# HGRN-2 decay levels: copies of the three widest levels moved to ScalarE, two levels formed in their valid blocks only

## The chip, the cores and the metric

The kernel runs on one core of a Trainium2 chip. The metric is the device time of one execution in microseconds. Three runs of the kernel before took 1720.81, 1721.70 and 1721.91 us (median 1721.7).

## The reference

Two blocks of a language model run over 256 tokens of width 1024 in float32: a Mamba-style mixer with a PEER layer, then a block with an HGRN-2 mixer, a convolutional FFN, windowed attention and a second FFN. The change lies in the HGRN-2 mixer. What it must compute, for each of 8 heads (q, k, v from the projections, `logf` the log of the forget gate):

```python
def step(state, inp):
    qb, kb, vb, gb = inp
    cum = jnp.cumsum(gb, axis=2)
    o_inter = jnp.einsum('bhtk,bhkv->bhtv', qb * jnp.exp(cum), state)
    rel = cum[:, :, :, None, :] - cum[:, :, None, :, :]
    decay = jnp.exp(jnp.where(causal, rel, -jnp.inf))
    scores = jnp.einsum('bhtk,bhsk,bhtsk->bhts', qb, kb, decay)
    o_intra = jnp.einsum('bhts,bhsv->bhtv', scores, vb)
    ...
```

So token t reads token s with the weight sum over k of q[t,k] k[s,k] exp(cum[t,k] - cum[s,k]).

## The kernel before

The 256 tokens are two tiles of 128. Scores are formed transposed (s on the partitions, t on the columns), as a hierarchy of **levels**, so that each exponent is taken against a reference point between s and t. Level 0 is the tile level: queries of tile 1 against keys of tile 0. Levels 1 to 7 have spans m = 64, 32, 16, 8, 4, 2, 1: within each run of 2m tokens the second half reads the first. Level 8 is the diagonal. They run in `LEVEL_ORDER` = 8, 0, 1, 2, ..., 7.

Work of one level x, on four engines that only meet at semaphores:

- **VectorE** `differences(x)` writes the exponents of the query side and the key side (two operations of 1024 columns, lines 2086 and 2088) into `QK[x % 2]`; it waits until TensorE has finished level x-2, which used the same buffer.
- **ScalarE** `level_exp(x)` takes both exponentials (lines 1970 and 1971).
- **VectorE** `q_side(x)` multiplies the query half by q (line 2123).
- **TensorE** `level(x)` (line 1855) forms a full 128x128 product for each of the 16 pairs of head and tile, though only the blocks of that level are valid, in banks 4 to 7, four to a bank; a float32 product shows as two matmul records. Level 0 is 8 products in banks 4 and 5 (line 1846). `bank_free` holds a bank until the level before has been copied out of it.
- **VectorE** `take(x)` (line 2139) copies each bank into `PP` under the mask of that level, four copies of 128x512; for level 0 it is two plain copies into `CR` (line 2132). Each adds to `level_out`.

Between the levels TensorE does slabs 2 to 13 of a weight stream, `wide(k)`: 12 matmuls of 512 columns (lines 320 to 322), tabled in `AFTER`. A slab comes from HBM into a ring of four and is split in two parts: **ScalarE** `split(k)` (line 239) writes the rounded high part of the slab that `wide(k + 3)` will use, **VectorE** `split(k)` (line 247) the rest. The high part of a slot may be overwritten only when TensorE has finished the slab that was there, so ScalarE's `split(k)` waits for the end of `wide(k - 1)`. At k = 8 ScalarE first copies four finished banks out (line 2005, `VT`), after `wide(7)`.

All queues are in order and written by hand. ScalarE's order per level x is: the splits up to `max(AFTER[x]) + 1`, then `level_exp(x + 2)`. VectorE's is: first split of `AFTER[x]`, `take(x)`, `q_side(x + 1)`, `differences(x + 2)`, remaining splits. When the last level is copied out, `read_out` (line 1877) forms the outputs.

Of the kernel before, what the change touches and what calls it, by code (L numbers as in the profile page):

```python
# [14 lines left out]
F32 = mybir.dt.float32  # L15
# [3 lines left out]
ACT = mybir.ActivationFunctionType  # L19
# [3 lines left out]
P = 128  # L23
# [108 lines left out]
def build(nc, t):  # L132
    ctx = ExitStack()
    with ctx:
# [16 lines left out]
        iota = sb("iota", P)  # L151
        tiny = sb("tiny", 64)
        arena = sb("arena", 32768)
        bank = [ctx.enter_context(nc.psum_tensor(f"bank{i}", [P, 512], F32)) for i in range(8)]

        def V(name, i=0, n=1):
            o = VEC[name][0]
# [147 lines left out]
                    last = short(k, k == KT - 1)  # L305
            last.then_inc(slabs_done, 1)

        def up_wide(pe, n0, k, bank_free=None):


            q = slot(n0 + k, 0)
            pe.wait_ge(lo_ready, n0 + k + 1)
            for tt in range(TT):
                x = slice(k * SEQ + tt * P, k * SEQ + (tt + 1) * P)
                for nh in range(2):
                    if bank_free is not None:
                        pe.wait_ge(bank_free, 2 * tt + nh + 1)
                    o = bank[2 * tt + nh][:, :]
                    w = slice(q * 1024 + nh * 512, q * 1024 + (nh + 1) * 512)
                    nc.tensor.matmul(o, xhi[:, x], whi[:, w], start=k == 0, stop=False)  # L320
                    nc.tensor.matmul(o, xhi[:, x], wlo[:, w], start=False, stop=False)
                    last = nc.tensor.matmul(o, xlo[:, x], whi[:, w], start=False, stop=k == KT - 1)  # L322
            last.then_inc(slabs_done, 1)

        def down_half(o, y, nh, q, first):

# [1487 lines left out]

        LEVEL_ORDER = (8, 0, 1, 2, 3, 4, 5, 6, 7)
        AFTER = {8: (2,), 0: (3,), 1: (4, 5), 2: (6, 7), 3: (8, 9), 4: (10,), 5: (11, 12), 6: (), 7: (13,)}
        PLACE_OF = {x: at for at, x in enumerate(LEVEL_ORDER)}

        def span_of(x):
            return ((P,) + LEVELS[:-1])[x]  # L1820

        def pe_hgrn(pe):
            turn_pe(pe, T_HG)
            up(pe, N_HG, U_HG, 0, 0, 4, SEQ, x_ready=lo_base(T_HG))
            steps(pe, 15, 4, lambda i, r: up(pe, N_HG + 1, U_HG + 1, i, r, 4, SEQ))

            def wide(k):
                up_wide(pe, N_HG + 16 + k // 8 * 8, k % 8, s("v_out") if k == 8 else None)

            def level(x):  # L1830

                before = LEVEL_ORDER[PLACE_OF[x] - 1] if PLACE_OF[x] else None
                if x < 8:
                    pe.wait_ge(s("qk_q"), x + 1)
                    pe.wait_ge(s("e_k"), x + 1)

                def bank_free(b):
                    if before is not None:
                        pe.wait_ge(s("level_out"), 4 * PLACE_OF[x] - 4 + (4 if before == 0 else b + 1))

                qk = QK[x % 2]
                if x == 0:
                    for hd in range(HG_H):
                        if hd % 4 == 0:
                            bank_free(hd // 4)
                        nc.tensor.matmul(bank[4 + hd // 4][:, (hd % 4) * P:(hd % 4 + 1) * P],
                                         qk[:, hd * SEQ:hd * SEQ + P], qk[:, hd * SEQ + P:(hd + 1) * SEQ],
                                         start=True, stop=True).then_inc(s("level_mm"), 2)
                    return
                for hc in range(2 * HG_H):  # L1850
                    if hc % 4 == 0:
                        bank_free(hc // 4)
                    q = slice(hc * P, (hc + 1) * P)
                    a, b = (KK[:, q], QQ[:, q]) if x == 8 else (qk[:, q], qk[:, q])
                    nc.tensor.matmul(bank[4 + hc // 4][:, (hc % 4) * P:(hc % 4 + 1) * P], a, b,  # L1855
                                     start=True, stop=True).then_inc(s("level_mm"), 1)

            pe.wait_ge(s("onr_in"), 16)
            nc.tensor.transpose(bank[7][:, 0:P], ONR, ident[:, :]).then_inc(s("onr_tr"), 1)
            pe.wait_ge(up_evac, U_HG + 16 + 2)  # L1860
            wide(0)
            wide(1)
            pe.wait_ge(s("q_silu"), 1)
            pe.wait_ge(s("onc"), 1)
            for x in LEVEL_ORDER:
                level(x)
                for k in AFTER[x]:
                    wide(k)
            pe.wait_ge(s("level_out"), 4 * 9)

            def read_out(half):
                for tt in range(TT):
                    for hd in range(4 * half, 4 * half + 4):
                        o = bank[4 + 2 * tt + half][:, (hd % 4) * P:(hd % 4 + 1) * P]
                        v = lambda c: VT[:, c * D + hd * P:c * D + (hd + 1) * P]
                        if tt == 0:
                            last = nc.tensor.matmul(o, PP[:, hd * SEQ:hd * SEQ + P], v(0), start=True, stop=True)
                        else:
                            nc.tensor.matmul(o, CR[:, hd * P:(hd + 1) * P], v(0), start=True, stop=False)
                            last = nc.tensor.matmul(o, PP[:, hd * SEQ + P:(hd + 1) * SEQ], v(1),  # L1880
                                                    start=False, stop=True)
                    last.then_inc(s("o_mm"), 1)

            def wide_last(nh):

                for z in range(2):
                    n = N_HG + 16 + 14 + z
                    q = slot(n, 0)
                    if nh == 0:
                        pe.wait_ge(lo_ready, n + 1)  # L1890
                    w = slice(q * 1024 + nh * 512, q * 1024 + (nh + 1) * 512)
                    for tt in range(TT):
                        x = slice((6 + z) * SEQ + tt * P, (6 + z) * SEQ + (tt + 1) * P)
                        o = bank[2 * tt + nh][:, :]
                        nc.tensor.matmul(o, xhi[:, x], whi[:, w], start=False, stop=False)
                        nc.tensor.matmul(o, xhi[:, x], wlo[:, w], start=False, stop=False)
                        last = nc.tensor.matmul(o, xlo[:, x], whi[:, w], start=False, stop=z == 1)
                        if nh and tt:
                            last.then_inc(slabs_done, 1)
                        elif z:  # L1900
                            last.then_inc(s("gate_mm"), 1)

            def turned_out(half):
                pe.wait_ge(s("o_gated"), 2 * half + 2)
                for j in (0, 2, 1, 3):
                    for tt in range(TT):
                        c = tt * D + (4 * half + j) * P
                        last = nc.tensor.transpose(turned_y(4 * half + j)[:, tt * P:(tt + 1) * P],
                                                   OO[:, c:c + P], ident[:, :])
                    if j > 1:  # L1910
                        last.then_inc(s("o_tr"), 1)

            read_out(0)
            read_out(1)
            wide_last(0)
            wide_last(1)
            turned_out(0)
            down(pe, N_HGO, D_HGO, 0, 0, 4, first=True)
            down(pe, N_HGO + 1, D_HGO + 1, 0, 0, 4)
            turned_out(1)  # L1920
            for j in (2, 3, 4, 5):
                down(pe, N_HGO + j, D_HGO + j, 0, 0, 4)
            down_last(pe, N_HGO + 6, D_HGO + 6)
# [7 lines left out]
        def act_hgrn(act, chain):  # L1931
# [69 lines left out]
            def slot_free(k):  # L2001
# [4 lines left out]
                            .then_inc(s("v_out"), 1)  # L2006
                split(k)

            level_exp(0)
            split(0)  # L2010
            split(1)
# [2 lines left out]
            for x in LEVEL_ORDER:  # L2014
                while done <= max(AFTER[x], default=0) + 1 and done < 14:
                    slot_free(done)
                    done += 1
                if x + 2 < 8:
                    level_exp(x + 2)
            split(14)  # L2020
# [14 lines left out]
        def dve_hgrn(dve, chain):  # L2035
# [90 lines left out]
            def take(x):  # L2126

                at = PLACE_OF[x]
                if x == 0:
                    for b in range(2):  # L2130
                        dve.wait_ge(s("level_mm"), 16 * at + 8 * (b + 1))
                        nc.vector.tensor_copy(CR[:, b * 512:(b + 1) * 512], bank[4 + b][:, :])\
                            .then_inc(s("level_out"), 2)
                    return
                for b in range(4):
                    dve.wait_ge(s("level_mm"), 16 * at + 4 * (b + 1))
                    if at:
# [13 lines left out]
            for x in LEVEL_ORDER:  # L2151
                if AFTER[x]:
                    split(AFTER[x][0])
                take(x)
                if x < 7:
                    q_side(x + 1)
                if x + 2 < 8:
                    differences(x + 2)
                for k in AFTER[x][1:]:
# [655 lines left out]
```

## Time and profile before

| | |
|---|---|
| median of three runs | 1721.7 us |
| the profiled execution: time, span | 1720.77 us, 1719.0 us |
| TensorE (PE) busy | 1671.2 us, 97% of the span |
| PE weight loads, VectorE, ScalarE, GpSimd busy | 88%, 75%, 60%, 6% |
| chain that ended last | PE 89%, VectorE 4%, ScalarE 4%, issue 2%, DMA 1% |
| level stage (first wide slab to first output product) | 1135.0 to 1207.7 us |

PE is TensorE's matmuls, PEld its weight loads, DVE VectorE, ACT ScalarE. PEclk is the granted clock of TensorE as a share of 2.4 GHz; 0.50 is 1.2 GHz. A matmul's recorded duration is longer than the distance to the next start, because matmuls are pipelined: costs are read from start to start. Idle time in brackets counts from the end of the record before.

### The profile page before, as it was taken

Reading aid. Unit: us, or ns where it says so; the run is one execution under the profiler, and the core shown is the slowest. Engines: PE = TensorE matmul, PEld = TensorE weight load, DVE = VectorE, ACT = ScalarE, POOL = GpSimd, SP = SyncE. Lnnn points to the kernel's source line nnn. Section 1 sums busy time; section 2 is a strip of 40 time slices with the busy share of each in tenths; the row PEclk is TensorE's granted clock in tenths of the full one; section 3 lists DMA queues with packets and bytes.
Section 4 is the critical chain, followed back from the end, with each engine's and each line's share of the span. In section 5 each row is a group of like instructions: output and inputs, shape, how many; then the busy total and the mean of one; then the engine's idle time right before and its main releaser. Section 6 shows DMA issues by size and latency. Waiting matters only on the chain.

```text
span 1719.0 us, 34329 instructions
## 1 busy us (share of the span) xinstructions
PE 1671.2 (97%) x10835; PEld 1505.5 (88%) x10835; DVE 1285.0 (75%) x2348; ACT 1031.7 (60%) x1615; POOL 109.7 (6%) x100
## 2 busy tenths in 40 slices
PE   7999999999999999999999999999999998999997
PEld 6998889999999999988888888898788887778886
DVE  6876773799967777777777777789677777867776
ACT  7656554667556666655445544764575667666655
POOL 0014300344100000000000000000000000000000
PEclk9999999999999999999999999999999999999999
DMA  5552356578765555577787777543356554246653
GB/s 201 165 157 94 107 181 211 174 223 230 230 213 169 180 170 178 164 233 241 244 273 239 242 243 239 171 148 99 123 172 190 191 193 140 87 147 196 188 191 109
DMA packets 113261, 315.62 MB, mean 184 GB/s; under 512 B 12624, under 2 KB 44752, under 8 KB 112688
## 3 DMA queue, kind: packets, MB, share of 16 engines
q1 hardware_dynamic: 112352, 310.83, 56.4%
q0 software_dynamic: 848, 4.00, 0.7%
q8 instruction: 35, 0.57, 0.1%
q14 instruction: 26, 0.21, 0.0%
HBM read 296.43 MB, written 18.35 MB: 183 GB/s over the span
## 4 chain that ended last, share of the span: by engine, by line
PE 89%; DVE 4%; ACT 4%; issue 2%; DMA 1%; ACTq 0%; DVEq 0%; SPq 0%
PE bank L263 11%; PE bank L264 11%; PE bank L265 11%; PE bank L328 10%; PE bank L329 10%; PE bank L330 10%; PE bank L284 9%; PE bank L288 5%; PE bank L1397 3%; PE bank L1855 1%; ACT whi L239 1%; DVE wlo L247 1%; PE bank L320 1%; PE bank L322 1%; DVE h L479 1%
## 5 line engine op out<-in xcount | busy, mean ns | idle before, releaser
L247 DVE TENSOR_TENSOR wlo<-raw,whi 128x1024 fp32r<-128x1024 f32 x500 | 614.5, 1231 | 145.7 <-ACT whi L239 136.1
L239 ACT ACTIVATE whi<-raw 128x1024 fp32r<-128x1024 f32 x524 | 550.5, 1052 | 40.4 <-PE bank L322 34.4
L263 PE MATMUL bank<-x,whi 128*128 128x256 f32 (+1 forms) x1728 | 507.5, 294 | 6.0 <-DVE arena L798 1.7
L265 PE MATMUL bank<-x,wlo 128*128 128x256 f32 (+1 forms) x1728 | 491.5, 284 | 0.0
L264 PE MATMUL bank<-x,whi 128*128 128x256 f32 (+1 forms) x1728 | 491.1, 284 | 0.0
L263 PEld LDWEIGHTS bank<-x,whi 128*128 128x128 f32 x1728 | 331.1, 192 | 11.1 <-issue 8.6
L264 PEld LDWEIGHTS bank<-x,whi 128*128 128x128 f32 x1728 | 331.8, 192 | 0.1
L265 PEld LDWEIGHTS bank<-x,wlo 128*128 128x128 f32 x1728 | 331.0, 192 | 0.0
L328 PE MATMUL bank<-whi,yhi 128*128 128x512 f32 x816 | 319.5, 392 | 4.9 <-DVE ylo L2340 2.0
L329 PE MATMUL bank<-wlo,yhi 128*128 128x512 f32 x816 | 318.1, 390 | 0.0
L330 PE MATMUL bank<-whi,ylo 128*128 128x512 f32 x816 | 317.5, 389 | 0.0
L328 PEld LDWEIGHTS bank<-whi,yhi 128*128 128x128 f32 x816 | 153.4, 188 | 38.5 <-issue 5.3
L330 PEld LDWEIGHTS bank<-whi,ylo 128*128 128x128 f32 x816 | 153.2, 188 | 32.4
L329 PEld LDWEIGHTS bank<-wlo,yhi 128*128 128x128 f32 x816 | 153.4, 188 | 29.4
L284 PE MATMUL bank<-x,whi 128*128 128x512 f32 x704 | 177.4, 392 | 1.0 <-DVE x L601 0.8
L1481 ACT ACTIVATE yhi<-h 128x256 fp32r<-128x256 f32 x128 | 53.4, 417 | 170.9 <-PE bank L330 167.2
L284 PEld LDWEIGHTS bank<-x,whi 128*128 128x128 f32 x704 | 129.2, 188 | 27.2 <-issue 1.2
L1434 ACT ACTIVATE h<-bank 128x256 f32<-128x256 f32 x128 | 49.2, 384 | 150.1 <-PE bank L265 149.9
L1675 DVE TENSOR_TENSOR ylo<-h,yhi 128x256 fp32r<-128x256 f32 x128 | 54.4, 425 | 66.8 <-ACT yhi L1481 66.8
L288 PEld LDWEIGHTS bank<-x,wlo 128*128 128x128 f32 x704 | 96.9, 190 | 6.9
L288 PE MATMUL bank<-x,wlo 128*128 128x256 f32 x704 | 100.2, 282 | 0.0
L1630 DVE TENSOR_SCALAR h<-iota,h 128x128 f32<-128x128 f32 x256 | 76.9, 343 | 22.9 <-PE bank L1397 22.9
(323 smaller groups left out, 1705.0 us busy)
## 6 DMA issues: line engine op xcount, KB each, us to landing
raw<-in_stream SPq DMA_DIRECT2D x524, 512.0 KB, 3.5
act_spill<-h SPq DMA_DIRECT2D x124, 128.0 KB, 3.2
h<-act_spill SPq DMA_DIRECT2D x124, 128.0 KB, 3.3
h<-in_x SPq DMA_DIRECT2D x1, 1024.0 KB, 5.3
arena<-in_keys POOLq DMA_DIRECT2D x1, 1024.0 KB, 6.5
h_spill<-h SPq DMA_DIRECT2D x1, 1024.0 KB, 8.4
arena<-h_spill POOLq DMA_DIRECT2D x1, 1024.0 KB, 7.8
arena<-in_g_final POOLq DMA_DIRECT2D x1, 512.0 KB, 9.3
```

What stands on the lines that cost most here:

```text
L239: nc.scalar.activation(whi[:, q * 1024:(q + 1) * 1024], raw[:, q * 1024:(q + 1) * 1024], ACT.Copy).then_inc(hi_ready, 1)
L247: nc.vector.tensor_tensor(wlo[:, q * 1024:(q + 1) * 1024], raw[:, q * 1024:(q + 1) * 1024], whi[:, q * 1024:(q + 1) * 1024].bitcast(F32), ...
L263: nc.tensor.matmul(bank[b][:, 0:T], whi[:, w], xhi[:, x], start=k == 0, stop=False)
L264: nc.tensor.matmul(bank[b][:, 0:T], whi[:, w], xlo[:, x], start=False, stop=False)
L265: last = nc.tensor.matmul(bank[b][:, 0:T], wlo[:, w], xhi[:, x], start=False, stop=k == KT - 1)
L284: return nc.tensor.matmul(bank[b][:, :], whi[:, w], both, start=k == 0, stop=k == KT - 1)
L288: return nc.tensor.matmul(bank[b][:, SEQ:2 * SEQ], wlo[:, w], xhi[:, k * SEQ:(k + 1) * SEQ], start=False, stop=stop, skip_group_check=True)
L328: nc.tensor.matmul(o, yhi[:, y], whi[:, w], start=first, stop=False, skip_group_check=True)
L329: nc.tensor.matmul(o, yhi[:, y], wlo[:, w], start=False, stop=False, skip_group_check=True)
L330: return nc.tensor.matmul(o, ylo[:, y], whi[:, w], start=False, stop=True, skip_group_check=True)
L1630: nc.vector.tensor_scalar(HOT1[:, y % 2 * P:(y % 2 + 1) * P], iota[:, :], c1(I1T), c1(GT_COLS), ALU.is_equal, ALU.mult).then_inc(s("hot_a" ...
L1675: nc.vector.tensor_tensor(ylo[:, yq * SEQ:(yq + 1) * SEQ], PRD[:, yq * SEQ:(yq + 1) * SEQ], yhi[:, yq * SEQ:(yq + 1) * SEQ].bitcast(F32), ...
```

## The change

- The eight PSUM banks become slices of one PSUM tensor, so that one access can span banks 4 to 7 (`SCORES`).
- Levels 1 (m = 64) and 2 (m = 32) are formed only in their valid blocks: per head and tile, level 1 is one product of 64 weight columns and 64 moved columns at output partitions 0 to 63; level 2 is two products of 32 by 32, at output partitions 0 and 64. Both wait for all four banks before they start.
- The copies of levels 0, 1 and 2 go from VectorE's queue to ScalarE's: two of 512 columns for level 0 as before, one of 64 partitions by 1024 elements for level 1, two of 32 partitions by 512 elements for level 2. In ScalarE's queue `take(x)` stands behind the splits of level x and ahead of `level_exp(x + 2)`.
- On VectorE `q_side(x + 1)` comes ahead of `take(x)`.
- The wide slabs are tabled by halves (`HALVES_AFTER`, 6 matmuls each). The order stays as it was except that the first half of `wide(11)` comes ahead of level 5.

```diff
+        HALVES_AFTER = {8: (4, 5), 0: (6, 7), 1: (8, 9, 10, 11), 2: (12, 13, 14, 15), 3: (16, 17, 18, 19),
+                        4: (20, 21, 22), 5: (23, 24, 25), 6: (), 7: (26, 27)}
+        SCORES = psum[:, 4 * 512:8 * 512].rearrange("p (c t) -> p c t", t=P)
 # pe_hgrn, level(x)
+                if x in (1, 2):
+                    m = span_of(x)
+                    bank_free(3)
+                    for hc in range(2 * HG_H):
+                        for c0 in range(0, P, 2 * m):
+                            k = qk[:, hc * P + c0:hc * P + c0 + m]
+                            q = qk[:, hc * P + c0 + m:hc * P + c0 + 2 * m]
+                            last = nc.tensor.matmul(SCORES[c0:c0 + m, hc, c0 + m:c0 + 2 * m], k, q,
+                                                    start=True, stop=True)
+                        last.then_inc(s("level_mm"), 1)
+                    return
 # pe_hgrn
             for x in LEVEL_ORDER:
                 level(x)
-                for k in AFTER[x]:
-                    wide(k)
+                for z in HALVES_AFTER[x]:
+                    wide(z // 2, (z % 2,))
 # act_hgrn
+            def take(x):
+
+                at = PLACE_OF[x]
+                if x == 0:
+                    for b in range(2):
+                        act.wait_ge(s("level_mm"), 16 * at + 8 * (b + 1))
+                        nc.scalar.activation(CR[:, b * 512:(b + 1) * 512], bank[4 + b][:, :], ACT.Copy)\
+                            .then_inc(s("level_out"), 2)
+                    return
+                m = span_of(x)
+                act.wait_ge(s("level_mm"), 16 * at + 16)
+                act.wait_ge(s("level_out"), 4 * at)
+                pp = PP.rearrange("p (c t) -> p c t", t=P)
+                for c0 in range(0, P, 2 * m):
+                    last = nc.scalar.activation(pp[c0:c0 + m, :, c0 + m:c0 + 2 * m],
+                                                SCORES[c0:c0 + m, :, c0 + m:c0 + 2 * m], ACT.Copy)
+                last.then_inc(s("level_out"), 4)
                 while done <= max(AFTER[x], default=0) + 1 and done < 14:
                     slot_free(done)
                     done += 1
+                if x < 3:
+                    take(x)
                 if x + 2 < 8:
                     level_exp(x + 2)
 # dve_hgrn
-                take(x)
                 if x < 7:
                     q_side(x + 1)
+                if x > 2:
+                    take(x)
                 if x + 2 < 8:
                     differences(x + 2)
```

## Rows read from the trace of the kernel before

**Rows 1.** The page: engines' busy time, and the chain that ended last.

```profile
PE 1671.2 (97%) x10835; PEld 1505.5 (88%) x10835; DVE 1285.0 (75%) x2348; ACT 1031.7 (60%) x1615; POOL 109.7 (6%) x100
PE 89%; DVE 4%; ACT 4%; issue 2%; DMA 1%; ACTq 0%; DVEq 0%; SPq 0%
```

**Rows 2.** Busy time of a stretch: us, PE, PEld, DVE, ACT, POOL, PEclk, DMA share.

```profile
1151.50:1207.60 56.10, 53.20 (x345) 47.60 (x345) 50.64 (x57) 24.67 (x26) 0.00 (x0) 1.00 0.31 101
```

**Rows 3.** Timeline of PE: start, us, line, tiles, count, idle before and its releaser.

```profile
1151.28 0.39 PE L322 MATMUL bank<-whi,x 128*128 128x512 f32 x1
1151.91 3.84 PE L1855 MATMUL bank<-arena 128*128 128x128 f32 x32 [0.24 <-DVE arena L2123]
1155.50 0.48 PE L320 MATMUL bank<-whi,x 128*128 128x512 f32 x1
...
1160.81 0.39 PE L322 MATMUL bank<-whi,x 128*128 128x512 f32 x1
1161.04 3.73 PE L1855 MATMUL bank<-arena 128*128 128x128 f32 x32
1164.53 0.48 PE L320 MATMUL bank<-whi,x 128*128 128x512 f32 x1
...
1169.88 0.39 PE L322 MATMUL bank<-whi,x 128*128 128x512 f32 x1
...
1186.42 3.84 PE L1855 MATMUL bank<-arena 128*128 128x128 f32 x32 [0.74 <-DVE arena L2123]
...
1201.24 3.84 PE L1855 MATMUL bank<-arena 128*128 128x128 f32 x32 [1.92 <-DVE arena L2123]
```

**Rows 4.** Timeline of VectorE in the same stage.

```profile
1155.18 2.62 DVE L2139 COPY_PREDICATED arena<-arena,bank 128x512 f32<-128x512 uint32 x4
1157.65 1.24 DVE L2123 TENSOR_TENSOR arena<-arena 128x1024 f32<-128x1024 f32 x1
1158.78 1.25 DVE L2086 TENSOR_TENSOR arena<-arena 128x1024 f32<-128x1024 f32 x1
```

**Rows 5.** Timeline of ScalarE in the same stage.

```profile
1151.76 1.06 ACT L239 ACTIVATE whi<-raw 128x1024 fp32r<-128x1024 f32 x1 [3.50 <-PE bank L322]
...
1161.30 1.06 ACT L239 ACTIVATE whi<-raw 128x1024 fp32r<-128x1024 f32 x1 [1.66 <-PE bank L322]
1162.26 1.04 ACT L1970 ACTIVATE arena<-arena 128x1024 f32<-128x1024 f32 x1
...
1170.31 2.06 ACT L2005 ACTIVATE arena<-bank 128x512 f32<-128x512 f32 x4 [1.60 <-PE bank L322]
1172.23 1.08 ACT L239 ACTIVATE whi<-raw 128x1024 fp32r<-128x1024 f32 x1
```

**Rows 6.** Timeline of PE elsewhere: narrow float32 matmuls (weights 128*64, and 24 moved columns).

```profile
97.32 0.52 PE L1017 MATMUL bank<-ident,arena 24*16 24x24 f32 x7
97.69 0.38 PE L1021 MATMUL bank<-arena,vec 24*128 24x24 f32 x2
...
146.37 0.39 PE L1106 MATMUL bank<-arena 128*64 128x128 f32 x4
146.59 0.38 PE L1104 MATMUL bank<-arena 128*64 128x128 f32 x2
146.81 0.38 PE L1106 MATMUL bank<-arena 128*64 128x128 f32 x2
```

**Rows 7.** Waits of PE elsewhere, and PEclk around them (columns of groups 3 and 2).

```profile
1082.96 1.94 PE L569 MATMUL bank<-ident,arena 128*128 128x128 f32 x8 [3.38 <-DVE arena L501]
1083.00:1084.00 1.00, 1.00 (x5) 1.00 (x6) 0.32 (x2) 0.58 (x3) 0.00 (x0) 0.50 0.00 0
1088.00:1089.00 1.00, 1.00 (x8) 1.00 (x8) 1.00 (x4) 1.00 (x3) 0.00 (x0) 0.73 0.06 16
...
1459.91 1.19 PE L2411 MATMUL bank<-ident,arena 128*128 128x128 f32 x6 [1.75 <-DVE arena L2576]
1460.00:1461.00 1.00, 1.00 (x7) 0.85 (x8) 1.00 (x4) 0.00 (x1) 0.00 (x0) 0.80 0.75 295
1463.00:1464.00 1.00, 1.00 (x7) 1.00 (x6) 0.88 (x1) 1.00 (x5) 0.00 (x0) 0.50 0.00 0
```

More of the change, by code:

```diff
@@ L153, in build @@
         arena = sb("arena", 32768)
-        bank = [ctx.enter_context(nc.psum_tensor(f"bank{i}", [P, 512], F32)) for i in range(8)]
+        psum = ctx.enter_context(nc.psum_tensor("bank", [P, 8 * 512], F32))
+        bank = [psum[:, i * 512:(i + 1) * 512] for i in range(8)]
         def V(name, i=0, n=1):
@@ L306, in up_halves, with up_wide @@
             last.then_inc(slabs_done, 1)
-        def up_wide(pe, n0, k, bank_free=None):
+        def up_wide(pe, n0, k, bank_free=None, tiles=range(TT)):
             q = slot(n0 + k, 0)
             pe.wait_ge(lo_ready, n0 + k + 1)
-            for tt in range(TT):
+            for tt in tiles:
                 x = slice(k * SEQ + tt * P, k * SEQ + (tt + 1) * P)
@@ L322, in up_wide @@
                     last = nc.tensor.matmul(o, xlo[:, x], whi[:, w], start=False, stop=k == KT - 1)
-            last.then_inc(slabs_done, 1)
+                if tt == TT - 1:
+                    last.then_inc(slabs_done, 1)
         def down_half(o, y, nh, q, first):
@@ L1825, in pe_hgrn, with wide @@
             steps(pe, 15, 4, lambda i, r: up(pe, N_HG + 1, U_HG + 1, i, r, 4, SEQ))
-            def wide(k):
-                up_wide(pe, N_HG + 16 + k // 8 * 8, k % 8, s("v_out") if k == 8 else None)
+            def wide(k, tiles=range(TT)):
+                up_wide(pe, N_HG + 16 + k // 8 * 8, k % 8, s("v_out") if k == 8 else None, tiles)
             def level(x):
@@ L2128, in take @@
                 at = PLACE_OF[x]
[L2129 to L2134, printed above, removed]
                 for b in range(4):
```

## The prediction

> **What bounds the kernel now.** I read the page first: TensorE is busy 97% of the span and carries 89% of the chain that ended last [rows 1]. So a microsecond of TensorE's work or waiting is a microsecond of the kernel, and work of another engine counts only where TensorE waits for it. Then the stretch from the end of wide(3) to the first output product [rows 2]: 56.1 us, clock at its full level (1.00, that is 2.4 GHz), TensorE busy 53.2, VectorE 50.6, ScalarE 24.7. Then TensorE's timeline, for who ends each wait [rows 3]. Levels 2, 3, 4 and 6 start without any; level 1 waits 0.24, level 5 0.74, level 7 1.92 us, each time for q_side on VectorE. Together 2.90 us: all that a lighter VectorE can give back here. Last, ScalarE's timeline [rows 5]: it has much free time, but its splits start only when TensorE has finished a wide slab (1151.28 + 0.39 = 1151.67, split at 1151.76; 1160.81 + 0.39 = 1161.20, split at 1161.30; 1169.88 + 0.39 = 1170.27, the VT copies at 1170.31). ScalarE is idle because it is blocked, and what stands behind a split in its queue is blocked too.
>
> **The change, part by part.**
>
> *VectorE gets lighter.* It loses two masked takes (2.47 us each: 1155.18 to 1157.65 in rows 4) and two plain copies, and q_side (1.13 us: 1157.65 to 1158.78) goes ahead of the take. This is worth what TensorE waited for it, 2.90 us at most.
>
> *The takes on ScalarE: this adds a wait.* Level x+1 may start only when take(x) is done, and take(x) now stands behind the splits of level x, the last of which waits for the end of the last wide slab before level x+1. Before, these takes ran on VectorE beside the wide slabs; now TensorE has nothing left to do when they start. A 1024-column operation of ScalarE takes 0.96 us start to start (1161.30 to 1162.26), a 512-column copy from PSUM 0.48 (1170.31 to 1172.23 for four) and 0.60 to its end, as the record of four is 2.06 us [rows 5]. A release takes some 0.05 us.
> - Level 1: split(4) at 1151.76, then 0.96, 0.48 and 0.60 end take(0) at 1153.80; level 1 starts at 1153.85 and not 1151.91. Idle 2.18 us in place of 0.24: **+1.94**.
> - Level 2: with E the end of wide(5), split(6) starts at E + 0.10, take(1) at E + 1.06; I take its 1024 elements as 1.08 us (0.60 + 0.48), so level 2 starts at E + 2.19. It started at once before: **+2.19**.
> - Level 3: the four VT copies start at E + 0.04 (E is the end of wide(7)), then 1.92 for them, 0.95 for split(8), 0.48 + 0.60 for take(2), 0.05: E + 4.04, where level 3 started at once: **+4.04**.
>
> Behind the waiting takes on ScalarE stand level_exp(2), (3) and (4), and q_side of the same levels on VectorE waits for these. They are ready before TensorE has done the level it is held at and the wide slabs behind it, so they cost nothing further.
>
> *The end of the stage.* With the first half of wide(11) (6 matmuls, 1.4 us: a quarter of 1155.50 to 1161.04 [rows 3]) ahead of level 5, and VectorE no longer late, level 5 doesn't wait: **-0.74**. Level 7 follows level 6 directly. With E the end of wide(12): split(13) at E + 0.10, the query exponential from E + 1.06 to E + 2.12, q_side(7) from E + 2.17 to E + 3.30, and level 7 needs the first bank of take(6): one copy is 2.62 less three times 0.62 [rows 4], 0.75, which ends at E + 4.05, level 7 starts at E + 4.1. Level 6 ends at E + 3.49. Idle 0.60 in place of 1.92: **-1.32**. The last take ends about 0.8 us before wide(13) does, so read_out isn't held. In all the waits go from 2.90 to 9.0 us: **+6.1**.
>
> *Narrow products.* A full level is 32 records in 3.49 us (1161.04 to 1164.53), 0.109 us each [rows 3]. With 64 weight columns and 128 moved ones a record still takes 0.11 us where all go to one half of the output partitions (two in 146.59 to 146.81), and 0.055 where both halves take turns (four in 146.37 to 146.59) [rows 6]. Level 1 moves 64 columns, half of that: 32 x 0.055 = 1.8 us, saves 1.7; from both sides 1.6 to 3.5. Level 2 has 64 records of 32 by 32. The dearest reading is that a record doesn't get cheaper than the 0.053 us of the 24-column ones (seven in 0.37 us), 3.5 us and nothing saved; the cheapest is a quarter of 0.109 each, 1.7 us. I take 0.031, 2.0 us, as those 24-column rows load 128 weight columns mostly: saves 1.5. Leaving the narrow layout twice may cost 0.1 each. Sum **-3.0**.
>
> The Trainium skill's page "TensorE: Matmul & The Clock Gate" (the section on 56 ns against 53.3) has start to start never under about 25 ns, and about 62 ns for every matmul where the sequencer decodes it. By the first level 2 would be 1.6 us, by the second 4.0 us, slower than the full level. The averages of 0.053 and 0.055 us in rows 6 lie under 62 ns, so the trace speaks against the second figure, for short bursts at least.
>
> *The clock.* TensorE's idle times get long. The trace has an idle of 3.38 us before 1082.96 after which the clock is 0.50 (1.2 GHz) until 1088.5, and one of 1.75 us before 1459.91 with 0.50 from 1460.6 to 1464.0 [rows 7]; but the 1.92 us before level 7 left it at 1.00 [rows 3]. What runs at 0.50 takes twice as long. The 4.0 us before level 3 are longer than the longest of these: I count on a fall. From the shorter stretch at 0.50 (3.4 us) it costs at most 1.7 us, less what of it is idle: **+1.6**; from the longer (5.5 us of work) up to 2.8. The two waits of 2.2 us lie between rows that fell and one that didn't: 0 to 1.7 each, half of that each: **+1.4**.
>
> *Nothing else.* One PSUM tensor in place of eight is the same memory, and the halves of wide slabs have the same matmuls. DMA is used 31% in this stretch [rows 2], and ring slots come free by the same splits.
>
> Sum: +6.1 - 3.0 + 1.6 + 1.4 = **+6.1 us**. The profiled execution, 1720.77 us with 1.8 us outside its span of 1719.0, would become 1726.9; it is 0.9 under the median of the three runs, so the median becomes **1727.8 us**.
>
> **Rivals.**
> - *The clock holds.* All three idles pass without a fall, as the 1.92 us did. +3.1, 1724.8 us: within 0.2%. For it speaks that row, against it the 4.0 us.
> - *Narrow products save nothing in level 2.* 1.5 us more: 1729.3 us; with a fall at every wait, up to 1731. For it: no row here has 32 weight columns. A page of the skill says the same of it (TensorEngine Tiling, "Instruction Overhead": few moved columns cost as much as some 60 cycles' worth), with the same 1729.3.
> - *Faster.* The takes on ScalarE aren't late, as that engine is free half the time: the waits vanish and the products shrink, -2.9 - 3.0, 1715.8 us. The place is the split ahead of each take. It decides as soon as TensorE's idle time over the stage stays under 2.9 + 3.0 = 5.9 us; I get 9.0 from starts of splits that the trace has, and the order in the queue is in the code. Only if those splits ran well before the slab's end could it be so, and they follow it by 0.1 us in every row.
> - *The change doesn't do what it says:* a copy in 16 short runs from PSUM is much slower than a plain one. Twice the price for take(1) and take(2) is +2.1, 1729.9 us.
>
> **How the numbers follow.** The forecast (a fall at level 3, and one or none at the short waits or two) 0.62; the clock holds 0.10; level 2 saves nothing 0.15; slow copies or falls everywhere 0.10; faster 0.03. A measurement of this kernel can tell about 0.2%, 3.4 us, from no change. The range reaches from just under the case without a fall to near the dearest, 1724.3 to 1730.8 us. Slower by over 0.2% has the forecast, the two dearer cases and nothing of the second: 0.87; within 0.2% 0.10; faster 0.03.
>
> **What the profile after would show.** Right: before levels 1, 2 and 3 idle times of TensorE near 2.2, 2.2 and 4.0 us released by ScalarE's copies; none before level 5, about 0.6 before level 7; ScalarE in the order split, take, exponentials; level 1 in 1.8 and level 2 in 2.0 us; a clock of 0.50 for some us after level 3 starts. Wrong: levels 1 to 3 starting within 1 us of the slab before, level 2 in 3.5 us or more, or a clock of 1.00 all along.

## The result, and the profile of the changed kernel

The changed kernel takes **1726.29 us**, the median of 7 runs (1725.23 to 1728.89), against 1721.53 of 7 runs of the kernel before (1718.9 to 1722.09): a ratio of 1.0029, 95% interval 1.002 to 1.0038. It is 4.8 us slower (3.4 to 6.5). The prediction was 1727.8 us, range 1724.3 to 1730.8. The profiled execution, 1728.89 us with a span of 1727.1, is the slowest of the seven.

The page: engines' busy time and the chain that ended last, to be read against [rows 1].

```profile
PE 1672.0 (97%) x10867; PEld 1505.7 (87%) x10867; DVE 1279.4 (74%) x2338; ACT 1033.8 (60%) x1620; POOL 109.6 (6%) x100
PE 89%; ACT 4%; DVE 4%; issue 2%; DMA 1%; ACTq 0%; DVEq 0%; SPq 0%
```

The page hides what happened. TensorE's busy time is 0.8 us up, though it computes less, and VectorE's is 5.6 us down, which doesn't show in the time. The stretch from the end of wide(3) to the first output product says more (columns: stretch, its length, then busy us of TensorE, weight loads, VectorE, ScalarE, GpSimd, granted clock, DMA share, GB/s):

```profile
1151.50:1215.60 64.10, 54.75 (x378) 48.12 (x377) 44.97 (x48) 27.50 (x31) 0.00 (x0) 0.89 0.27 89
```

Against [rows 2] it is 8.0 us longer. TensorE's busy time rose only 1.5 us, its idle time from 2.9 to 9.35 us, and the clock fell to a mean of 0.89. The timeline of TensorE (start, duration, line, tiles, count, idle time before and its releaser), to be read against [rows 3]:

```profile
1151.50 0.39 PE L323 MATMUL bank<-whi,x 128*128 128x512 f32 x1
1154.16 2.58 PE L1863 MATMUL bank<-arena 128*64 128x64 f32 x32 [2.27 <-ACT arena L2032]
1156.67 0.80 PE L321 MATMUL bank<-whi,x 128*128 128x512 f32 x1
...
1165.63 1.92 PE L1863 MATMUL bank<-arena 128*32 128x32 f32 x64 [2.20 <-ACT arena L2040]
...
1173.57 0.39 PE L323 MATMUL bank<-whi,x 128*128 128x512 f32 x1
1178.18 5.99 PE L1872 MATMUL bank<-arena 128*128 128x128 f32 x32 [4.22 <-ACT arena L2040]
...
1197.19 3.73 PE L1872 MATMUL bank<-arena 128*128 128x128 f32 x32
...
1209.28 3.81 PE L1872 MATMUL bank<-arena 128*128 128x128 f32 x32 [0.65 <-DVE arena L2170]
```

Levels 1, 2 and 3 wait 2.27, 2.20 and 4.22 us, each for a copy on ScalarE. Level 5 (1197.19) doesn't wait, level 7 waits 0.65. The timeline of ScalarE shows why, against [rows 5] (L240 is a split, L2032 take(0), L2040 take(1) and take(2), L2022 the VT copies, L1987 an exponential):

```profile
1151.98 1.06 ACT L240 ACTIVATE whi<-raw 128x1024 fp32r<-128x1024 f32 x1 [3.50 <-PE bank L323]
1152.95 1.06 ACT L2032 ACTIVATE arena<-bank 128x512 f32<-128x512 f32 x2
...
1163.53 1.06 ACT L240 ACTIVATE whi<-raw 128x1024 fp32r<-128x1024 f32 x1 [1.67 <-PE bank L323]
1164.49 1.00 ACT L2040 ACTIVATE arena<-bank 64x1024 f32<-64x1024 f32 x1
...
1174.00 2.07 ACT L2022 ACTIVATE arena<-bank 128x512 f32<-128x512 f32 x4 [1.60 <-PE bank L323]
1175.92 1.08 ACT L240 ACTIVATE whi<-raw 128x1024 fp32r<-128x1024 f32 x1
1176.87 1.17 ACT L2040 ACTIVATE arena<-bank 32x512 f32<-32x512 f32 x2
```

ScalarE sits idle 3.50, 1.67 and 1.60 us until TensorE ends a wide slab (L323). Only then come the split (with the VT copies ahead of it at level 3) and, last, the copy that TensorE wants. The level starts within 0.15 us of that copy's end (1176.87 + 1.17 = 1178.04, level 3 at 1178.18).

And the clock, in windows of 1 us (columns as above):

```profile
1156.00:1157.00 1.00, 1.00 (x8) 0.88 (x8) 0.44 (x2) 0.00 (x0) 0.00 (x0) 0.50 1.01 410
1167.00:1168.00 1.00, 1.00 (x22) 0.92 (x17) 1.00 (x2) 0.38 (x1) 0.00 (x0) 0.50 0.77 250
1176.00:1177.00 1.00, 0.00 (x0) 0.00 (x0) 0.00 (x0) 1.00 (x3) 0.00 (x0) 0.50 0.54 217
1182.00:1183.00 1.00, 1.00 (x8) 1.00 (x7) 0.70 (x1) 0.00 (x0) 0.00 (x0) 0.63 0.00 0
```

In this execution the clock was at 0.50 (1.2 GHz) for a while with each of the three waits: it fell after the first two, and during the third (the window from 1176.00 has no matmul and is at 0.50). Before, it stayed at 1.00 in this stretch [rows 2]. This is why level 3 lasts 5.99 us and not 3.84, and a matmul of a wide slab 0.80 us and not 0.48.

### The profile page after: what moved, and what is told of

It reads as the page before. It is cut to its first block, busy times and chain, and to the rows that moved or that the text cites. A ratio compares the mean times of both kernels' runs of the same rounds, so it can differ in the third digit from the quotient of the medians.

```text
span 1727.1 us, 34383 instructions
## 1 busy us (share of the span) xinstructions
PE 1672.0 (97%) x10867; PEld 1505.7 (87%) x10867; DVE 1279.4 (74%) x2338; ACT 1033.8 (60%) x1620; POOL 109.6 (6%) x100
## 4 chain that ended last, share of the span: by engine, by line
PE 89%; ACT 4%; DVE 4%; issue 2%; DMA 1%; ACTq 0%; DVEq 0%; SPq 0%
PE bank L264 11%; PE bank L265 11%; PE bank L266 11%; PE bank L330 10%; PE bank L331 10%; PE bank L332 10%; PE bank L285 9%; PE bank L289 5%; PE bank L1399 3%; PE bank L1872 1%; PE bank L321 1%; PE bank L322 1%; PE bank L323 1%; ACT whi L240 1%; DVE wlo L248 1%
## 5 line engine op out<-in xcount | busy, mean ns | idle before, releaser
L240 ACT ACTIVATE whi<-raw 128x1024 fp32r<-128x1024 f32 x524 | 550.6, 1052 | 48.0 <-PE bank L323 41.7
L264 PEld LDWEIGHTS bank<-x,whi 128*128 128x128 f32 x1728 | 331.1, 192 | 11.3 <-issue 8.5
```

What stands on the lines that cost most here:

```text
L240: nc.scalar.activation(whi[:, q * 1024:(q + 1) * 1024], raw[:, q * 1024:(q + 1) * 1024], ACT.Copy).then_inc(hi_ready, 1)
L264: nc.tensor.matmul(bank[b][:, 0:T], whi[:, w], xhi[:, x], start=k == 0, stop=False)
```

## The experiments

Times stand against the kernel before on the same chip; its medians there lay from 1720.96 to 1721.71 us. "Stage" is the time from the start of level 8 to the first output product in the profiled execution: **67.1 us before, 74.9 after**.

### 1. The takes ahead of the splits

All of the change stays; the three takes on ScalarE only move ahead of the splits, and take(0) also waits for the take of level 8.

```diff
                 if x == 0:
+                    act.wait_ge(s("level_out"), 4 * at)
 ...
             for x in LEVEL_ORDER:
+                if x < 3:
+                    take(x)
                 while done <= max(AFTER[x], default=0) + 1 and done < 14:
                     slot_free(done)
                     done += 1
-                if x < 3:
-                    take(x)
```

> The changed kernel, but in ScalarE's queue take(x) stands ahead of the splits of level x and not behind them (take(0) also waits for all of take(8)). Theory (the loss is the takes' place behind splits that wait for the end of a wide slab): the takes run beside the wide slabs, TensorE's idle times before levels 1, 2 and 3 (2.27, 2.20, 4.22 us) go to about 0, the clock doesn't fall there, level 7 still waits about 0.8 us. Against the changed kernel -8.3 us of waiting and about -3 us of clock, so about 1715.5 us, some 6 us faster than before. Rival A (the narrow products or the changes of array layout are what costs): little moves, 1724 to 1727 us. Rival B (copies in short runs on ScalarE are slow by themselves): at most a few us of gain, about 1722 us, with a wait left before levels 2 and 3.

Measured: **1713.92 us** (1711.8 to 1715.96, 5 runs), ratio 0.9955 (0.9941 to 0.9968), stage 60.85 us. TensorE's timeline:

```profile
1152.18 2.08 PE L1863 MATMUL bank<-arena 128*64 128x64 f32 x32
1154.18 0.50 PE L321 MATMUL bank<-whi,x 128*128 128x512 f32 x1
...
1159.85 1.21 PE L1863 MATMUL bank<-arena 128*32 128x32 f32 x64
1160.98 0.50 PE L321 MATMUL bank<-whi,x 128*128 128x512 f32 x1
1166.57 3.73 PE L1872 MATMUL bank<-arena 128*128 128x128 f32 x32
...
1195.61 3.81 PE L1872 MATMUL bank<-arena 128*128 128x128 f32 x32 [0.83 <-DVE arena L2171]
```

The three waits are gone and the clock is 1.00 in these stretches. But for the wait that take(0) got, nothing else differs from the changed kernel, so the place of three copies in ScalarE's queue is worth 0.74% or 12.7 us (some 10 to 15 by the two intervals): 8.5 of it waiting (9.34 to 0.83); the other 4.2 lie near the 3.1 that experiment 4 gives for the clock. This is the rival "faster" of the prediction, which came true as soon as its condition was made true.

The same rows give the price of the narrow products at full clock: level 1 takes 2.00 us to the next product (1152.18 to 1154.18), level 2 takes 1.13 (1159.85 to 1160.98), where a full level takes 3.49 [rows 3]. Together they save 6.98 - 3.13 = 3.85 us.

A group hides one thing that only the single records of the trace show. In level 1, whose products all go to output partitions 0 to 63, the records start 58.3 ns apart. In level 2, whose products go in turn to partitions 0 to 31 and 64 to 95, they start in pairs: some 7 ns within a pair (1 to 3 in experiment 2), 31.7 ns from pair to pair, in all six traces that have this level at full clock. Read with the code, each half of the output takes a record every 31.7 ns, and the two halves run side by side; that is how 64 records fit into 1.13 us. [rows 6] had the same: 0.055 us where two halves take turns, 0.11 where one is used.

### 2. Only take(2) ahead

```diff
             for x in LEVEL_ORDER:
+                if x == 2:
+                    take(x)
                 while done <= max(AFTER[x], default=0) + 1 and done < 14:
 ...
-                if x < 3:
+                if x < 2:
                     take(x)
```

> The changed kernel, but only take(2) goes ahead of its splits (and so ahead of the four VT copies and split(8)). Theory: only the wait before level 3 goes (4.22 us), and with it one fall of the clock (about 1.6 us); those before levels 1 and 2 stay at 2.2 us: about 1720.7 us. If a fall of the clock costs nothing: 1722.2 us. Rival A (narrow products): 1726 us.

Measured: **1720.71 us** (1718.33 to 1722.77, 10 runs), ratio 0.9996 (0.9986 to 1.0005), stage 66.9 us:

```profile
1154.64 3.50 PE L1863 MATMUL bank<-arena 128*64 128x64 f32 x32 [2.27 <-ACT arena L2032]
...
1166.01 1.21 PE L1863 MATMUL bank<-arena 128*32 128x32 f32 x64 [2.20 <-ACT arena L2040]
...
1172.75 3.73 PE L1872 MATMUL bank<-arena 128*128 128x128 f32 x32
```

Each wait hangs on its own take: the third is gone, the first two are there to the hundredth. After the first the clock fell (level 1 takes 3.50 us), after the second, as long, it didn't (1.21 us). A wait of 2.2 us is thus a case where either happens, as the prediction had it.

### 3. Full products in levels 1 and 2

```diff
-                if x in (1, 2):
+                if False:
```

> The changed kernel with levels 1 and 2 formed as full 128x128 products again; ScalarE still copies only the valid blocks. Theory: the narrow products save about 3.0 us of TensorE's time and the waits don't depend on them, so this is about 3 us slower than the changed kernel: 1729.3 us, with the same waits of 2.2, 2.2 and 4.2 us. Rival A (narrow products save nothing or cost): 1726.3 us or less.

Measured: **1733.22 us** (1731.52 to 1734.17, 4 runs), ratio 1.0071 (1.0056 to 1.0087). This missed by 4 us: undoing the narrow products costs 7 us over the changed kernel, not 3. Its waits are the same; two of the three levels behind them run partly at low clock:

```profile
1154.83 3.81 PE L1872 MATMUL bank<-arena 128*128 128x128 f32 x32 [2.27 <-ACT arena L2032]
...
1166.31 5.44 PE L1872 MATMUL bank<-arena 128*128 128x128 f32 x32 [2.20 <-ACT arena L2040]
...
1181.45 5.38 PE L1872 MATMUL bank<-arena 128*128 128x128 f32 x32 [4.22 <-ACT arena L2040]
```

It left open whether the narrow products are worth 3.85 us and the rest is clock, or whether they are worth 7. Experiments 4, 5 and 7 tell that.

### 4. Unread matmuls in the waits

The changed kernel, with 2, 2 and 4 products of data at hand, which nobody reads, in a free bank ahead of levels 1, 2 and 3. They fill the waits without ending them sooner.

```diff
+                if x in (1, 2, 3):
+                    lo, hi, n = {1: (64, P, 2), 2: (64, P, 2), 3: (32, 64, 4)}[x]
+                    for i in range(n):
+                        nc.tensor.matmul(bank[7][lo:hi, :], KK[:, lo:hi], QQ[:, 0:512], start=True, stop=True)
 ...
                 level(x)
+                if x == 0:
+                    pe.wait_ge(s("level_out"), 4)
```

> The changed kernel with matmuls that nobody reads in the waits before levels 1, 2 and 3 (2, 2 and 4 products of 64 or 32 by 512 into partitions of bank 7 that hold no valid block; about 1.7, 1.7 and 3.4 us, less than each wait). The levels start when they did. Theory: the falls of the clock after these waits cost about 3 us in the middle of the runs, so with the clock held at 1.00 it takes about 1723.3 us, with less spread between runs. If the clock costs nothing here: 1726.3 us. If narrow fill matmuls don't hold the clock: also 1726.3 us, with 0.50 in the same places of the profile.

Measured: **1723.22 us** (1720.61 to 1724.37, 11 runs), ratio 1.0011 (1.0001 to 1.002). The fillers (L1851) and the levels behind them:

```profile
1151.62 1.93 PE L1851 MATMUL bank<-arena 128*64 128x512 f32 x4
1153.87 2.08 PE L1867 MATMUL bank<-arena 128*64 128x64 f32 x32 [0.32 <-ACT arena L2038]
...
1163.73 1.21 PE L1867 MATMUL bank<-arena 128*32 128x32 f32 x64 [0.25 <-ACT arena L2046]
...
1170.53 3.62 PE L1851 MATMUL bank<-arena 128*32 128x512 f32 x8
1174.73 3.84 PE L1876 MATMUL bank<-arena 128*128 128x128 f32 x32 [0.58 <-ACT arena L2046]
```

Filler and rest of the wait together are as long as the wait was (1.93 + 0.32 = 2.25 us; 3.62 + 0.58 = 4.20), and level 3 is back at 3.84 us, the clock at 1.00. So the difference to the changed kernel, 1.0029 - 1.0011 = 0.0018 or **3.1 us**, is what the clock falls cost; the two intervals together leave some 1 to 5 us. The mean granted clock of all runs says the same: 0.992 over the changed kernel's seven, 0.995 over these eleven and over the kernel before.

### 5. Narrow products alone

The kernel before, with levels 1 and 2 formed in their valid blocks; every copy is still a masked one on VectorE, as before.

```diff
+                if x in (1, 2):
+                    m = span_of(x)
+                    for hc in range(2 * HG_H):
+                        if hc % 4 == 0:
+                            bank_free(hc // 4)
+                        for c0 in range(0, P, 2 * m):
+                            k = qk[:, hc * P + c0:hc * P + c0 + m]
+                            q = qk[:, hc * P + c0 + m:hc * P + c0 + 2 * m]
+                            o = bank[4 + hc // 4][c0:c0 + m, (hc % 4) * P + c0 + m:(hc % 4) * P + c0 + 2 * m]
+                            last = nc.tensor.matmul(o, k, q, start=True, stop=True)
+                        last.then_inc(s("level_mm"), 1)
+                    return
```

> The kernel before, with only levels 1 and 2 formed in their valid blocks; all copies stay masked and on VectorE. Theory: with takes on VectorE no wait is added. Levels 1 and 2 take 2.0 and 1.1 us (as with the takes ahead of the splits) in place of 3.49 each, 3.85 us less, but VectorE is then late by about 1 us at level 3 (a new wait): about -2.8 us, 1718.2 us. Rival (the narrow form costs something that the copies on ScalarE hid): 1721 us or more. If VectorE paces the whole stage, the gain is under 1 us.

Measured: **1717.28 us** (1717.03 to 1720.57, 11 runs), ratio 0.9981 (0.9972 to 0.999), stage 64.1 us. The levels take 2.08 and 1.21 us as in experiment 1, and VectorE, now with less cover, comes late at level 3:

```profile
1167.37 3.84 PE L1867 MATMUL bank<-arena 128*128 128x128 f32 x32 [0.65 <-DVE arena L2135]
```

3.85 - 0.65 = 3.2 us, and the ratio gives 3.3 (1.7 to 4.8 by its interval). So the products are worth 3.85 us, not 7.

### 6. The query product ahead of the copies, alone

The kernel before, with q_side one place up on VectorE.

```diff
-                take(x)
                 if x < 7:
                     q_side(x + 1)
+                take(x)
```

> The kernel before, with only q_side(x + 1) ahead of take(x) on VectorE. Theory: the waits for q_side before levels 1, 5 and 7 (0.24, 0.74, 1.92 us) shrink, that before level 7 to about 0.8 us (it then waits for the first bank of take(6)): -1 to -2 us, 1719.0 to 1720.0 us. Rival (TensorE then waits for the take instead, as much as it did for q_side): 1721 us.

Measured: **1718.45 us** (1716.32 to 1719.37, 11 runs), ratio 0.9982 (0.9973 to 0.9991), stage 65.0 us. Level 5 waits no longer, level 1 0.34 us, level 7 now for the take itself:

```profile
1197.00 3.81 PE L1855 MATMUL bank<-arena 128*128 128x128 f32 x32 [0.80 <-DVE arena L2139]
```

The waits went from 2.90 to 1.14 us and the stage shrank by 2.1. The ratio gives 3.1 us (1.5 to 4.6), a little more than was expected; the trace accounts for 2.1 of it. Level 5 doesn't wait here, though no half of `wide(11)` was put ahead of it: the earlier q_side was enough for that. Each of the two other parts of the change is thus a gain of its own; the copies behind the splits undo both.

### 7. Full products with the waits filled

Experiments 3 and 4 together: the same two edits.

> The changed kernel with matmuls in the waits and full 128x128 products in levels 1 and 2. Theory (full products cost 3.85 us, and what the kernel with full products and no fill lost beyond that, 3.1 us, was the clock): 1723.2 + 3.85 = 1727.1 us, with the clock at 1.00 in the stage. Rival (full products cost 7 us for another reason): 1730 us.

Measured: **1726.93 us** (1726.41 to 1728.45, 5 runs), ratio 1.0036 (1.0022 to 1.005), waits left of 0.32, 0.25, 0.58 and 0.66. Against experiment 4 that is 3.7 us for the full products with the clock held. Against experiment 3 it is 6.3 us less by the medians, 6.0 by the ratios, with the same waits, filled or not: that is the clock, and the mean granted clock of its four runs, 0.991 against 0.995 here, fits (0.4% of 1730 us is some 7 us). With 3.1 us for the clock in experiment 4, the miss of experiment 3 would then be some 3 us more of low clock, and not the price of the products.

That the clock costs more with full products isn't shown, though. By the ratios, undoing the narrow products costs 0.0042 without fillers and 0.0025 with them, a difference of 0.0017 or 2.9 us, while the four intervals together leave about 4 us to either side. And the profiled executions say the opposite: with full products the stage is 76.8 us unfilled and 73.4 filled, 3.4 us of clock; in the changed kernel 74.9 and 69.45, 5.4 us. With full products only two of the three waits brought a fall of the clock, in the changed kernel all three.

### 8. Level 3 narrow as well

Experiment 1, with level 3 also formed in valid blocks (16 by 16) and taken by ScalarE in four copies of 16 partitions.

```diff
-                if x in (1, 2):
+                if x in (1, 2, 3):
 ...
-                if x < 3:
+                if x < 4:
                     take(x)
 ...
-                if x > 2:
+                if x > 3:
                     take(x)
```

> The kernel with the takes ahead of the splits, and level 3 (span 16) too formed in its valid blocks (4 products of 16 by 16 per head and tile) and copied by ScalarE (4 copies of 16 partitions by 256). Theory: VectorE isn't what holds TensorE, so only TensorE's own time counts: 128 records; at the 0.017 us per record of level 2 it is 2.2 us in place of 3.49, so -1.2 us, 1712.7 us. If a record costs 0.03 us or more, or the four short copies hold level 4 up: 1714 us or slower.

Measured: **1712.97 us** (1709.93 to 1713.41, 5 runs), ratio 0.9946 (0.9933 to 0.996), stage 58.7 us.

```profile
1166.52 1.51 PE L1863 MATMUL bank<-arena 128*16 128x16 f32 x128
1167.96 0.50 PE L321 MATMUL bank<-whi,x 128*128 128x512 f32 x1
...
1193.37 3.81 PE L1872 MATMUL bank<-arena 128*128 128x128 f32 x32 [0.68 <-DVE arena L2171]
```

Level 3 takes 1.44 us (1166.52 to 1167.96) for 3.49. Its saving is smaller than that of level 2, though the valid work halves again: 128 records need 0.0113 us each, 64 needed 0.0177. Its products go in turn to four parts of the output. The first 32 records start at four in 25 ns, the later ones at four in 46 ns on average; what slows them isn't known. The intervals of this kernel and of experiment 1 overlap, so the gain rests on the stage, 2.1 us shorter.

### 9. A half slab in the last wait

```diff
-                        4: (20, 21, 22), 5: (23, 24, 25), 6: (), 7: (26, 27)}
+                        4: (20, 21, 22), 5: (23, 24, 25), 6: (26,), 7: (27,)}
```

> The kernel three_narrow with one more half product of the next stage (26 of the list of halves) started between levels 6 and 7 instead of after level 7, to stand in the 0.7 us wait of level 7 for the masked take on VectorE. Theory (a wait at this point of TensorE's order is paid in full, and work put in it takes it away): level 7 waits 0 to 0.1 us instead of 0.68 us, and the time is 0.5 to 0.7 us under three_narrow, about 1712.3 us. Rival (the wait only moves: the last take then stands behind the half product's own evacuation and read_out waits for it): a wait of about 0.7 us shows at the first product of read_out, and the time is that of three_narrow, 1713.0 us. Second rival: the half product's evacuation gets ahead of the take on its engine and the wait at level 7 grows, 1713.5 us or more.

Measured: **1712.15 us** (1709.66 to 1713.24, 5 runs), ratio 0.9941 (0.9927 to 0.9955), stage 57.8 us.

```profile
1193.95 3.73 PE L1872 MATMUL bank<-arena 128*128 128x128 f32 x32
...
1198.91 1.05 PE L1894 MATMUL bank<-arena 128*128 128x128 f32 x8
```

Neither level 7 nor the first output product (L1894) waits: the wait didn't move, it is gone, and both rivals fall. The stage is 0.9 us shorter by the traces; the two times alone couldn't show it, as their intervals overlap. From 1152 to 1200 us TensorE is now busy all the time at full clock, and the next gain there has to come from its work (columns as in the stretch of the changed kernel):

```profile
1152.00:1200.00 48.00, 48.00 (x483) 42.26 (x483) 41.39 (x44) 28.72 (x34) 0.00 (x0) 1.00 0.35 118
```
Of all kernels this one has the lowest median: 0.59% under the kernel before, 0.88% under the changed one.

## Why the prediction was right, point by point

- **What bounds.** TensorE, and of the others only what it waits for: right. VectorE lost 5.7 us of work in the stretch, and only the 2.90 us that TensorE had waited for it could count.
- **The takes behind the splits.** Predicted were idle times of 2.18, 2.19 and 4.04 us, measured 2.27, 2.20 and 4.22. The starts and lengths of splits and copies from [rows 5] were enough. The third is 0.18 longer because the two copies of 32 partitions take 1.17 us, not 1.08, and its release 0.14, not 0.05.
- **The end of the stage.** Level 5 without a wait, level 7 with 0.60: measured none and 0.65. In all the waits rose by 9.34 - 2.90 = 6.4 us for +6.1.
- **Narrow products.** The term was mis-sized, -3.85 us for -3.0. Level 1 was taken at 1.8 and is 2.0 us; level 2 was taken at 2.0, between 1.7 and 3.5, and is 1.13 us, outside both ends. The 0.031 us per record was, as it happens, right for one half of the output (31.7 ns, experiment 1). What the prediction left out is that level 2 uses two halves in turn: it had read from [rows 6] that this halves the price of a record, and then counted 64 records of 0.031 one behind the other. Its cheapest case, 64 times a quarter of 0.109, leaves this out too. The 24-column rows [rows 6] were no good neighbours either: their 0.053 us is a mean of unlike records. Single records of the trace show two of the seven with 16 weight columns, followed after 28 and 25 ns, and the rest with 128, followed after 61 to 65.
- **The rule on small matmuls.** The Trainium skill's "TensorE: Matmul & The Clock Gate" (on 56 ns against 53.3) has no start-to-start time under about 25 ns. Averaged over all records, levels 2 and 3 need 17.7 and 11.3 ns. But within one part of the output, as read in experiments 1 and 8, a record of level 2 follows after 31.7 ns and one of level 3 after 25 at the least, which agrees. By matmul (each leaves two records) it is 35 and 23 ns, both under the 62 ns that the section has for decoding in the sequencer. "TensorEngine Tiling (Array Packing)" of the Trainium skill, "Instruction Overhead", has one column take as long as 60. Counted in columns the trace doesn't bear that out, as in one part of the output 32 columns take 31.7 ns and 64 take 58.3. Its 60 cycles would be 25 ns at 2.4 GHz (an estimate from that page's figure), and the records here are no shorter. The rival that level 2 saves nothing is refuted either way, by its 1.13 us.
- **The clock.** +3.0 us was predicted, a fall at the 4.0 us wait and every other time at those of 2.2. Experiment 4 gives 3.1, with some 1 to 5 by the intervals, so that the term was met to the tenth is luck. Its working has a slip too: half of 1.7 for each of two waits is 1.7, not 1.4. The profiled execution had all three falls; that fits its lying 2.6 us over the median, but its other executions have no profile.
- **The sum.** The parts as measured are 6.4 - 3.85 + 3.1 = 5.7 us; the times say 4.8 (3.4 to 6.5), the prediction said 6.1. Two of its errors partly cancel: 0.3 us too little for the waits, 0.85 too little for the products. With the clock held the first two alone make 2.6 us, and experiment 4 has 1.9 (0.2 to 3.4).
- **The rivals.** "The clock holds" doesn't hold in the trace, and experiment 4, where the clock is made to hold, gives what it promised: about 2 us over the kernel before, where that rival said 3. Slow copies: 1.00 us for the 16-run copy of take(1), as a plain one. "Faster" failed for the reason given: the splits follow the slab's end within 0.1 us, and the takes stood behind them.

What stays open: why the same wait of 2.2 us let the clock fall at level 1 and not at level 2 in experiment 2; whether the clock costs more behind full products, as experiment 3's profiled execution, the fastest of its four, shows only 3.4 us of it in the stage where the medians of experiments 3 and 7 differ by 6.3; and whether ScalarE is the right engine for the three copies at all. No run has the narrow products and the earlier q_side together with the copies left on VectorE. Experiments 5 and 6 alone add up to 0.37% under the kernel before, experiment 1 has 0.45%, and the intervals don't tell these apart.

## What to carry to other kernels

A copy that is moved to a less busy engine inherits that engine's queue: ask not how busy the engine is but what the instruction ahead of it waits for. "TensorEngine Tiling (Array Packing)" of the Trainium skill, "PSUM Bottleneck", advises to use both ScalarE and VectorE for taking results out of PSUM; here the kernel with the same copies on ScalarE is 0.29% slower than before where they stand behind the splits, and 0.45% faster where they stand ahead. Price an idle time of TensorE above its own length: about 8.7 us of waits brought some 3 us of slower work after them. And when a row of a timeline stands for many records, look at the single ones before taking its mean as a price: here one mean of 0.053 us held records of 25 and of 65 ns.

## What the runs showed of the hardware

- Float32 products in narrow column tiles: 32 records of 64 columns in 2.0 us, 64 of 32 in 1.13, 128 of 16 in 1.44, where a full level of 32 records of 128 takes 3.49. Start to start a record takes 111.7 ns at 128 columns and 58.3 at 64, where one part of the output is used. With 32 columns and two parts in turn, two records start every 31.7 ns; with 16 columns and four parts, four in 25 ns at first and in 46 later. So the fall from level 1 to level 2 comes from using two parts of the output, as both move 2048 columns in all.
- Waits of 2.2 us went with a clock of 0.50 in some cases (four of six in the profiled executions) and not in others, that of 4.2 us with 0.50 in both profiled executions that had it unfilled. Matmuls whose result nobody reads kept it at 1.00 in the same waits; the time fell by 3.1 us in the changed kernel and by some 6 with full products, which the intervals don't tell apart. It is a repair of the symptom: moving the copies brought 12.7.
